# A ring of ten weight slots with a table of their order, in a two-layer decoder trunk on one core

## The reference

```
for layer in (0, 1):
    h = rms_norm(x, norm_mix_g[layer])
    x = x + mixer(h)              # h @ w_in (1024 x 3072), attention, @ w_out (1024 x 1024)
    h = rms_norm(x, norm_ffn_g[layer])
    x = x + hier_moe(h)           # each token: best of 4 groups, then the 2 best of its 4 experts

# hier_moe, for each of the 16 experts e, on the tokens that chose it:
y = (silu(xb @ w_gate[e]) * (xb @ w_up[e])) @ w_down[e]    # three 1024 x 1024 matrices
out[token] += weight[token, e] * y
```

## Time and profile before

| stretch (us) | what runs | PE busy | DMA share | GB/s |
|---|---|---|---|---|
| 0 to 97 | layer 0, norm and input projection | 82.24 us | 0.73 | 255 |
| 97 to 155 | layer 0, attention, part of w_out | 48.75 us | 0.28 | 109 |
| 155 to 180 | layer 0, rest of w_out, router | 22.78 us | 0.56 | 224 |
| 180 to 640 | layer 0, experts; layer 1's norm | 437.94 us | 1.00 | 420 |
| 640 to 690 | layer 1, input projection | 50.00 us | 0.53 | 188 |
| whole span, mean | | 1156.8 us (94%) | | 356 |

### The profile page before, as it was taken

The page is one execution under the profiler, slowest core; times in us unless marked ns, Lnnn a source line. Parts: engine busy times, 40 slices in busy tenths (PEclk is TensorE's granted clock), DMA queues, the critical chain, the costliest instruction groups (busy, mean ns, idle before and its releaser), DMA issues.

```text
span 1235.4 us, 13941 instructions
## 1 busy us (share of the span) xinstructions
PE 1156.8 (94%) x5646; PEld 550.5 (45%) x5646; DVE 422.8 (34%) x748; ACT 189.8 (15%) x374; POOL 7.2 (1%) x36
## 2 busy tenths in 40 slices
PE   5997999999999999989979989899999999999897
PEld 4895453333333333333369854433333333333332
DVE  2655253232222322222265672532223222222223
ACT  3326311000000100000044161100000000000000
POOL 2000000000000000000000000000000000000000
PEclk9999999999999999999999999999999999999999
DMA  9665059999999999999995450899999999999995
GB/s 328 196 276 205 1 205 412 418 419 431 427 430 428 430 427 430 427 430 428 421 365 187 152 205 1 358 429 416 421 428 429 428 428 430 428 429 428 429 428 240
DMA packets 53904, 439.30 MB, mean 356 GB/s; under 512 B 14192, under 2 KB 14192, under 8 KB 29296
## 3 DMA queue, kind: packets, MB, share of 16 engines
q1 hardware_dynamic: 53872, 438.85, 85.8%
HBM read 437.79 MB, written 1.05 MB: 355 GB/s over the span
## 4 chain that ended last, share of the span: by engine, by line
PE 75%; DMA 18%; DVE 4%; ACT 2%; issue 1%; POOL 1%; DVEq 0%; POOLq 0%; SPq 0%; ACTq 0%
PE bank L1475 42%; DMA ring<-in_moe_w_up 11%; PE bank L1373 8%; DMA ring<-in_moe_w_gate 6%; PE bank L1413 4%; PE bank L1453 4%; PE bank L1487 4%; PE bank L1368 3%; PE bank L1463 1%; PE bank L1519 1%; PE bank L1292 1%; PE bank L1203 1%; PE bank L1512 1%; PE bank L1383 1%; PE bank L1243 1%
## 5 line engine op out<-in xcount | busy, mean ns | idle before, releaser
L1475 PE MATMUL bank<-ring,qkT 128*64 128x512 f32 x2944 | 653.1, 595 | 27.9 <-DMA ring<-in_moe_w_gate 15.4
L1475 PEld LDWEIGHTS bank<-ring,qkT 128*64 128x64 f32 x2944 | 204.4, 137 | 452.4 <-issue 406.3
L1167 DVE TENSOR_SCALAR qkT<-qkT 128x512 f32<-128x512 f32 x32 | 13.7, 428 | 484.6 <-ACT qkT L742 484.6
L1169 DVE RECIPROCAL qkT<-qkT 128x512 f32<-128x512 f32 x32 | 107.3, 3353 | 1.1
L1487 PE MATMUL bank<-qkT 64*128 64x512 f32 x256 | 63.6, 615 | 5.6 <-ACT qkT L747 5.6
L1174 DVE TENSOR_TENSOR qkT<-bank,qkT 128x512 f32<-128x512 f32 x32 | 22.1, 692 | 131.5 <-PE bank L1475 131.5
L747 ACT ACTIVATE qkT<-bank 128x512 f32<-128x512 f32 x32 | 19.1, 597 | 304.4 <-PE bank L1475 304.4
L1413 PE MATMUL bank<-ring,hn 128*128 128x512 f32 x128 | 55.7, 593 | 1.2 <-ACT hn L657 0.7
L742 ACT ACTIVATE qkT<-bank 128x512 f32<-128x512 f32 x32 | 19.1, 598 | 241.4 <-PE bank L1475 241.4
L932 DVE TENSOR_TENSOR w_low<-ring,w_high 128x2048 fp32r<-128x2048 f32 x22 | 49.4, 2286 | 11.6 <-ACT w_high L590 11.6
L1453 PE MATMUL bank<-fn_high,take 128*128 128x512 f32 x136 | 45.9, 419 | 2.8 <-DVE take L1057 2.8
(11 more groups left out here) (214 smaller groups left out, 867.4 us busy)
## 6 DMA issues: line engine op xcount, KB each, us to landing
ring<-in_moe_w_gate SPq DMA_DIRECT2D x64, 2048.0 KB, 22.0
ring<-in_moe_w_down SPq DMA_DIRECT2D x64, 2048.0 KB, 24.8
ring<-in_moe_w_up SPq DMA_DIRECT2D x56, 2048.0 KB, 24.3
ring_spare<-in_moe_w_up SPq DMA_DIRECT2D x8, 2048.0 KB, 26.3
ring<-in_ab_w_in SPq DMA_DIRECT2D x12, 1024.0 KB, 14.2
ring<-in_c_w_in SPq DMA_DIRECT2D x12, 1024.0 KB, 14.4
ring<-in_ab_w_out SPq DMA_DIRECT2D x2, 2048.0 KB, 15.2
ring<-in_c_w_out SPq DMA_DIRECT2D x2, 2048.0 KB, 15.4
```

Of the source, the lines that this page charges most:

```text
L1169: nc.vector.reciprocal(sig, sig).then_inc(s.gate_step, 1)
L1475: last = mm(b[SLOTS * half:SLOTS * (half + 1), :], left(h, k), expert_rhs(slot, k, half), start=(h == 0 and k == 0), stop=(h == 1 and k == ...
```

## The change

Line numbers of the changed file are 6 or 7 higher. Four things change.

1. The ring has ten slots instead of nine: nine of their own memory (0 to 8) and the spare, now slot 9.
2. The order of slots is a table, `SLOT_OF_UNIT`. Units 0 to 9 of a quad take slots 0 to 9 in order. Units 10 to 23 take slots 2, 3, 4, 5, 0, 1, 6, 7, 2, 3, 4, 5, 8, 9.
3. Ahead of the loop one more unit is loaded: unit 8 goes to slot 8 right behind `w_out`, without a wait. The spare slot now gets unit 9 at `logits_psum`, and the loop starts with unit 10.
4. The memory for it (16 KB on each partition) comes from the descriptor scratch, which is set to 1024 bytes, and from the forget gate's tables, which now lie over `bias_a`.

```
-RING = 8
+RING = 9
 SPARE = RING
 QUAD = 4
 QUAD_UNITS = QUAD * UNITS
 
-PLACES = [(SPARE, 0) if i == RING else ((i - (i > RING)) % RING, (i - (i > RING)) // RING)
-          for i in range(QUAD_UNITS)]
+SLOT_OF_UNIT = [*range(RING + 1), 2, 3, 4, 5, 0, 1, 6, 7, 2, 3, 4, 5, 8, 9]
+PLACES = [(slot, SLOT_OF_UNIT[:i].count(slot)) for i, slot in enumerate(SLOT_OF_UNIT)]
...
         w_high = [rounded(f"w_high{i}", [P, NC, COLS], ring_at[UNITS + i])
-                  for i in range(RING - UNITS)]
+                  for i in range(2)]
...
         bias_a = sb("bias_a", [P, A_HEADS, SW], BF16)
+        bias_at = nc.sbuf_base - 2 * A_HEADS * SW
+
+        def over_bias(name, n, at):
+
+            return nc.alloc_sbuf_tensor_at(name, [96, n], BF16, offset=bias_at + at)
...
-        cum = [sb(f"cum{i}", [96, T], BF16) for i in range(3)]
-        cum_neg = sb("cum_neg", [96, SW], BF16)
+        cum = [over_bias(f"cum{i}", T, 2 * T * i) for i in range(3)]
+        cum_neg = over_bias("cum_neg", SW, 6 * T)
...
                 load_wout(layer)
+                load_unit(layer, RING - 1, RING - 1 - UNITS, 1)
                 sp.wait_ge(s.out_psum, 4 * layer + 4)
-                for slot in range(UNITS, RING):
+                for slot in range(UNITS, RING - 1):
                     load_unit(layer, slot, slot - UNITS, 1)
...
-    nc = bacc.Bacc("TRN2", target_bir_lowering=False, num_devices=1)
+    nc = bacc.Bacc("TRN2", target_bir_lowering=False, num_devices=1, dynamic_dma_scratch_size=1024)
```

## The result

Six runs of the changed kernel have a median of 1241.11 us (1239.95 to 1243.18), six of the kernel before 1235.82 us (1233.87 to 1238.1). The ratio is 1.0033 with a 95% interval of 1.0016 to 1.0049: some 4 us slower (2 to 6 us), and within the half per cent that was called no change. The two medians are 5.3 us apart; this text goes by the ratio and its interval. The profiled execution took 1240.15 us, against 1237.52 before.

A forecast was written before the change was run, and what follows sets the result against it. The stream of unit transfers, through unit 93's landing, was taken to set each layer's end. Layer 0 (+3.5 - 1.7 + 0.5 = +2.3) and layer 1 (+4.0 - 2.6 + 0.5 = +1.9) gave +4.2 us: 1242, range 1236 to 1247.

The forecast's parts named there:

- The stream sets the end: Expert stages: unit 93's landing sets each layer's end, one for one, up to 9.7 us of gain a layer.
- Unit 8 gains nothing in the end: Ahead of the loop: the 4.9 us won by loading unit 8 early are lost in a hole of 10 us.
- The rival of the extra unit in full: Both layers' streams become one unit shorter: -9.8 us, about 1228; chance 0.08.
- The first transfer of the loop: Unit 10 waits for unit 2, is issued at 193.24 and takes 7.9 us: +3.5 us in layer 0, +4.0 in layer 1.
- Losses given back: Stream up to unit 93: losses apart from the disturbances go, 1.7 us in layer 0 and 2.6 in layer 1.
- The stall at unit 18: Layer 0: 1.5 us lost to a short queue before the change; it should go, with unit 18 issued well ahead.
- the table's later slots: From unit 10 on: real leads of eight to ten places, so the losses of 1.7 and 2.6 us should go.
- Unit 12's short place: Unit 12 waits for slot 4, issued only 3.3 us before unit 11 lands: +0.5 us a layer, bounds 0 and 1.5.
- The disturbances: Late landings at unit 14 in layer 0 (0.9 us) and unit 12 in layer 1 (1.0), not tied to short queues: kept.
- The sum: Layer 0 +2.3 and layer 1 +1.9, together +4.2 us, so 1242; bounds +1.3 and +10.5.
- Memory and `w_in`: Tables over `bias_a`, new addresses and the next layer's earlier `w_in`: 0 each; rival that the smaller scratch is felt: 0.02.

The follow-up runs named there:

- D: The changed kernel with passes of 48 units and its ten slots used in turn, no lead below nine: 0.9935 to the kernel before, 1228.92 us.
- B: The kernel before with passes of 48 units and its nine slots each used in turn: 1.000 to the kernel before, 1237.43 us.
- A: The kernel before with passes of 48 units and its old order of nine slots written twice, a control: 1.0027, 1241.7 us.

## Why the prediction was right

The forecast was 1242 us and no measurable change; the median is 1241.11. Point by point:

- *The stream sets the end.* Shown: 9.4 us more of a hole made unit 93 9.7 and 9.2 us later and cost 20 us in two layers. A hole that was nearly closed, with better later leads, gave 5.6 and 6.6.
- *Unit 8 gains nothing in the end.* Shown by the run with unit 8 late, 1.0038 for 1.0033. The rival of the extra unit in full fell for the reason given: only slot 2's release can start unit 10. The extra slot in itself is worth something: with an order in turn it gave 8 us (D against B).
- *The first transfer of the loop.* Predicted issue 193.24 with 7.9 us to landing. Measured 191.29, or 193.9 with the 2.60 us of the earlier start put back, and 8.1 us: unit 10 lands 4.4 us later than before (199.4 + 2.6 against 197.6), where +3.5 stood. In layer 1 it landed at 809.25; less the 2.21 of the later start, 4.1 us behind the 803.0 of before, and +4.0 stood.
- *Losses given back.* Predicted, net of unit 12: 1.2 and 2.1 us. Measured 4.4 - 2.44 = 2.0 and 4.1 - 2.05 = 2.0. The landings (issue and us to landing of each unit; the changed kernel on the clock of the kernel before, +2.60 in layer 0 and -2.21 in layer 1) show where:

| unit | layer 0: before | changed | later by | layer 1: before | changed | later by |
|---|---|---|---|---|---|---|
| 10 | 197.6 | 202.0 | 4.4 | 803.0 | 807.0 | 4.1 |
| 13 | 212.3 | 217.2 | 4.8 | 818.5 | 823.0 | 4.4 |
| 14 | 218.1 | 222.0 | 4.0 | 823.4 | 827.8 | 4.4 |
| 17 | 232.7 | 236.8 | 4.0 | 838.1 | 842.6 | 4.5 |
| 18 | 239.2 | 241.7 | 2.5 | 844.0 | 847.6 | 3.6 |
| 23 | 263.6 | 266.1 | 2.5 | 868.7 | 872.0 | 3.3 |
| 24 | 268.6 | 271.0 | 2.4 | 874.9 | 876.9 | 2.0 |

  The stall at unit 18 went, as predicted: its issue at 226.56 is 7.6 us ahead of unit 17's landing (234.15), and it lands 4.9 us behind it. That gave 1.5 us in layer 0 and 0.9 in layer 1. In layer 1 a gap of 6.2 us ahead of unit 24, which the prediction hadn't found, went too and gave 1.3. From unit 24 to unit 93 (2.44 and 2.05 us later) nothing more is won or lost, so the table's later slots cost nothing. The size of the stall isn't a constant: in five stages with the old order it was 0.9 to 2.0 us, and in a sixth, layer 0 of A, there was none.
- *Unit 12's short place, 0.5 each.* In layer 0 no stall of it can be found. In layer 1 unit 12 came 1.2 us late; before the change it was 0.9 late there too. It may be the same disturbance; but its issue at 810.85 was only 3.3 us ahead of unit 11's landing (814.16), which is the prediction's own condition for a short queue. The two causes aren't separated.
- *The disturbances* were kept in the sum at full size. In layer 0 that was too much: unit 14 lands 4.9 us behind unit 13 in the changed kernel, and 0.4 us are lost at unit 13 instead of 0.9 at unit 14. That and the 0.5 of unit 12 make up the 0.8 that layer 0 gave back beyond the forecast, to within the scatter. A possible cause of the disturbances is this: the window of 208 to 216 us in the kernel before, in which unit 14 was delayed, holds a packet of the instruction queue.

```profile
q1 hardware_dynamic: 229, 3.41, 100.0%
q8 instruction: 1, 0.02, 0.8%
```

  The transfer that came late in the changed kernel, unit 13's (209.2 to 214.5), holds such a packet too. It fits, and the 48-unit passes with their many fetches are slower, but no run took a single fetch away: this is not shown.
- *The sum.* +2.3 and +1.9 predicted, +2.4 and +2.1 in the profiles, 4.1 us (2 to 6) in the ratio.
- *Memory and `w_in`.* Zero each; the first is shown to within -2.5 to +1.2 us, the second was not tried by itself.

The time of 1241 comes from the right steps, and part of the closeness is luck: two terms of layer 0 were off by nearly the same amount in opposite directions (0.9 too little for the first transfer, 0.8 too little given back), single layers scatter by up to 0.9 us where no wait was moved, and the medians of the kernel before itself lie between 1235.8 and 1238.5 from one set of runs to the next.

## What to carry to other kernels

In this kernel a larger ring helped only when its slots were used in turn where the consumer (here TensorE) has just begun. The transfer that first depends on the consumer sets the pace of the whole stream. Each microsecond of emptiness that was added ahead of it was paid at the end, in spite of eight units in stock, because the consumer comes to wait for the stream later on. When a table must repeat after a number of places that the slots don't divide, put the short leads where the queue is long, and write the first pass out apart. An early transfer ahead of a transfer that waits for the consumer only lengthens the pause.

## What the runs showed of the hardware

- With passes of 48 units the instruction queue, on the same DMA engines as the data, has 9 packets in every pass (run A); in the kernel before, with passes of 24, it has 4 early in each expert stage, and none from 304 to 625 or from 900 to 1100 us. Over the run these are 49 packets of 16 KB against 21 or 22, and 29 with the first pass apart. The control with the longer pass cost 3.3 us (0.6 to 6), and its TensorE paused 4.7 and 10.4 us at the turn, which its stock covered.
- The same matmuls cost different amounts from one execution to the next: 14.08 or 16.55 us for 64 of them at the start, with a granted clock of 1.00 in both; 3.68 or 6.09 us for 8 transposes, with a granted clock of 1.00 or 0.50. Two profiles of an identical stage can differ by 2.6 us at its start; compare from the start of the stage.
- A transfer of 2048 KB that finds the engines empty takes 7.7 to 8.1 us from issue to landing, against 4.89 a unit in the stream.
